# Order of the token tiles in layer 0's attention: context tiles between latent tiles

## The reference, cut to what matters

```python
for l in range(DEPTH):
    need_ctx = l < DEPTH - 1            # DEPTH = 2: layer 0 alone
    ...
    mix_x, mix_c = _token_mixers(px, pc, ...)
    h_x = _layer_norm(ALPHA * h_x + ga_x * (mix_x @ w_out[l]), ...)
...
# _token_mixers
o_a = _window_attn_latent(...)          # keys: 128 to either side, and the context, and a sink
o_b = _global_attn_latent(...)          # keys: all
o_d = _neigh_attn_latent(...)           # keys: all, with bias and mask
mix_c = concatenate([_dense_attn(a...), _dense_attn(b...), oc_ctx, _dense_attn(d...)])
```

## Time and profile before

| | |
|---|---|
| median of three runs | 2217.05 us |
| the profiled execution | 2221.32 us, its span 2219.5 us |
| busy share of the span | PE 92%, DVE 60%, ACT 33%, POOL 37% |
| attention of layer 0 | 453.1 us to 594.9 us |
| mean granted TensorE clock | 0.95 of full speed |

### The profile page before, as it was taken

One profiled execution on the slowest core, in us unless ns is written; L12 is line 12 of the kernel. 1 busy time (PEld: TensorE's weight loads), 2 busy tenths in 40 slices (PEclk: granted clock), 3 DMA queues, 4 the chain that ended last, 5 costly groups with the idle time before them and its releaser, 6 DMA issues.

```text
span 2219.5 us, 30665 instructions
## 1 busy us (share of the span) xinstructions
PE 2039.5 (92%) x11900; PEld 1641.9 (74%) x11900; DVE 1332.1 (60%) x2690; ACT 742.3 (33%) x1412; POOL 813.7 (37%) x620
## 2 busy tenths in 40 slices
PE   6998999989894999999989989999899969999897
PEld 3665877867682888888878867676777748888786
DVE  1028868676568799999843261875866762222445
ACT  2113343256611222222243311332336523333442
POOL 0005455220144243333353331444420354555553
PEclk9999998999996999999999999999799979999898
DMA  7541010110010333333321111111010102222321
GB/s 294 188 172 39 20 39 20 39 53 2 25 53 19 133 114 124 124 114 114 133 76 67 48 57 57 39 39 39 20 72 1 52 26 95 95 95 95 113 86 67
DMA packets 24128, 169.80 MB, mean 77 GB/s; under 512 B 2608, under 2 KB 2608, under 8 KB 4784
## 3 DMA queue, kind: packets, MB, share of 16 engines
q1 hardware_dynamic: 22544, 157.87, 19.7%
q10 hardware_dynamic: 1440, 9.96, 1.1%
HBM read 165.72 MB, written 2.10 MB: 76 GB/s over the span
## 4 chain that ended last, share of the span: by engine, by line
PE 76%; DVE 12%; issue 5%; POOL 4%; ACT 2%; DMA 1%; SPq 0%; POOLq 0%; DVEq 0%; ACTq 0%
PE PS L954 27%; PE PS L912 17%; PE PS L728 10%; PE PS L722 6%; PE PS L849 3%; PE PS L874 3%; PE PS L833 2%; PE PS L764 2%; DMA WR<-in_weights 1%; PE PS L839 1%; PE PS L649 1%; POOL W L1747 1%; DVE H L1611 1%; DVE H L1609 1%; PE PS L861 1%
## 5 line engine op out<-in xcount | busy, mean ns | idle before, releaser
L954 PE MATMUL PS<-XH,WS 128*128 128x512 f32 (+1 forms) x2112 | 571.4, 357 | 10.0 <-POOL WS L1785 6.9
L954 PEld LDWEIGHTS PS<-XH,WS 128*128 128x128 f32 x2112 | 378.5, 190 | 68.1 <-issue 9.7
L954 PE MATMUL PS<-XL,WS 128*128 128x512 f32 (+1 forms) x1056 | 376.1, 356 | 0.0
L1785 POOL TENSOR_TENSOR WS<-WR,WS 128x1024 fp32r<-128x1024 f32 x88 | 212.3, 2413 | 361.9 <-ACT WS L1163 361.9
L728 PE MATMUL PS<-WR,X 128*128 128x256 f32 x1248 | 290.5, 394 | 5.2 <-DMA WR<-in_weights 5.2
L728 PEld LDWEIGHTS PS<-WR,X 128*128 128x128 f32 x1248 | 245.4, 199 | 43.0 <-DMA WR<-in_weights 6.2
L1174 ACT ACTIVATE W<-PS,PR 128x768 f32<-128x768 f32 (+1 forms) x88 | 78.0, 886 | 464.5 <-PE PS L954 400.0
L954 PEld LDWEIGHTS PS<-XL,WS 128*128 128x128 f32 x1056 | 201.3, 191 | 28.2
L722 PE MATMUL PS<-X,WR 128*128 128x512 f32 (+1 forms) x576 | 209.1, 520 | 10.3 <-ACT U L1026 6.8
L1668 DVE SCALAR_TENSOR_TENSOR W<-PS,PR,W 128x511 f32<-128x511 f32 (+1 forms) x132 | 83.0, 656 | 217.1 <-ACT W L1174 217.1
L1250 DVE SCALAR_TENSOR_TENSOR W<-WR,SC,W 128x256 f32<-128x256 f32 x336 | 191.2, 610 | 6.0
(11 more groups left out here) (180 smaller groups left out, 3458.7 us busy)
## 6 DMA issues: line engine op xcount, KB each, us to landing
WR<-in_weights SPq DMA_DIRECT2D x144, 1024.0 KB, 4.8
W<-in_ln_rows ACTq DMA_DIRECT2D x4, 1024.0 KB, 4.6
U<-in_bias ACTq DMA_DIRECT2D x2, 1792.0 KB, 9.6
H<-in_x SPq DMA_DIRECT2D x1, 2048.0 KB, 10.4
WR<-in_weights SPq DMA_DIRECT2D x4, 512.0 KB, 3.5
out_h<-H ACTq DMA_DIRECT2D x4, 512.0 KB, 2.6
H<-in_ctx SPq DMA_DIRECT2D x1, 1024.0 KB, 12.5
PR<-in_params SPq DMA_DIRECT2D x1, 624.0 KB, 3.5
```

Source lines behind the costliest of these rows:

```text
L954: mm = pe.matmul(PS[u.pos][:, lo:hi], w[:, part, k, :], src[:, k, lo:hi], start=(k == 0 and src is xh3 and part == 0), stop=(k == KT - 1 a ...
L1785: pool.tensor_tensor(ws5[:, u.c % 2, 1], half_slot(u), ws5[:, u.c % 2, 0], ALU.subtract).then_inc(w_low, 1)
```

## The change

In layer 0 the tiles of each group are taken in the order 0, 4, 1, 5, 2, 3 instead of 0, 1, 2, 3, 4, 5. Layer 1 keeps its order.

```diff
         for l in range(DEPTH):
             for g in "ABD":
-                for t in range(tiles(l)):
+                for t in (0, 4, 1, 5, 2, 3) if has_ctx(l) else range(NLT):
                     for p in range(2):
```

## The result

The new order is slower: 2229.61 us, the median of six runs (2225.08 to 2231.45), against 2217.43 us (2216.51 to 2220.53, six runs). The ratio is 1.0050, with a 95% interval of 1.0038 to 1.0063, which is 11 us more, between 8.4 and 14; the medians themselves lie 12.2 us apart. I had forecast +3.2 us, at most 2223.5. The direction holds, the size doesn't, and what I called "can't be told from no change" can be told well.

The account below looks back on a forecast made before the run. TensorE, 92% busy, was taken to bound the kernel, with one large hole ended by GpSimd's L1758. 5.2 - 1.5 + 1.1 - 0.5 - 1.1 = +3.2 us gave 2220.3 us, range 2216.0 to 2223.5.

Parts of the forecast that it names:

- The wall: Layer 0, group A: VectorE's L1531, with two SBUF inputs, gets through only when GpSimd's L1758 lets go.
- the release: Group A: the moment GpSimd's L1758 lets VectorE's L1531 through, 8.29 us after L1515, ahead of the roots of job 5.
- T: End of the second L1508 in group A, 469.55 before, forecast 468.1; roots of job 5 start at T + 14.18.
- Work moved behind the release: Group A: scores, transposes and values of TensorE that ran ahead of the release now run behind it, +5.2 us.
- the release earlier: Group A: two context jobs instead of latent ones on VectorE bring T forward, -1.5 us, between 0 and 2.1 earlier.
- Seams, +1.1: Passages from a context tile to a latent one, groups A, B, D: 2.0 us new less 0.9 old.
- twice that: Upper bound set on the cost of seams from context to latent tiles, forecast between 0 and twice +1.1 us.
- Seams that go and the drain: Context pairs behind tile 4 no longer wait for maxima, -0.5 us; attention ends on latent tiles with less idleness, -1.1.
- The clock: The slow spell behind the release stays at about 1.4 us in both orders: 0, up to +1.5 us.
- slower by the clock: Rival, group A: clock falls to 1.2 GHz ahead of T, sum +4.7 to +6.9 us, from 2221.8; 13%.
- Everything behind attention is shifted and nothing else: Work after layer 0's attention only moves in time; layer 1 must look the same.
- slower by over 0.2%: Whole kernel: a time from 2221.5 us on, made of clock, L1515 late, part of the seams and the forecast's upper edge; 30%.

Follow-up runs that it names:

- Group A alone: The new order only in group A of layer 0, against the kernel before: ratio 1.0036 (1.0023 to 1.0049), attention 146.15 us, +4.3.
- late scaling: GpSimd's scaling of the bias table waits until group A's last sums are formed: 2210.24 us with the old order, 2215.10 us with the new.
- short exponentials: New order, late scaling, layer 0 group B exponentials over 64 columns without the maximum: 2215.15 us against 2215.10 with full ones; attention 140.26 against 141.57.
- run 20: Not a label of a run: part of "could run 20 us later", a verb and a time, said of an instruction on GpSimd.

## Why the prediction was wrong, step by step

- *The wall* (the release hangs on the second L1508 alone): right. 14.18 us from T to the roots in both orders, and without GpSimd's scaling beside it L1531 takes 0.16 us.
- *Work moved behind the release, +5.2; the release earlier, -1.5*: right. Group A alone cost +4.3 where the two, its seams and the clock sum to 4.1. From the roots of job 5 to L900 the new order takes 120.42 us against 111.19, 9.2 more; the moved work, the clock, the seams as measured below and the two gains at the end sum to 9.05.
- *Seams, +1.1*: the failed step. By distances in TensorE's rows the seams behind the release cost 0.6 in A, 3.2 in B and 1.9 in D, 5.7, where I had 2.0. Less the 0.9 of the old order's seams this is +4.8 and not +1.1. Two errors: I priced only the entry to a latent tile and nothing for the exit of a lone one, and in B's entry I let the waiting head take half of a pair's time, when alone it takes nearly all of it. My upper bound, "twice that", had the same blind spot: both rows it came from are seams with a second latent tile behind them, where the exit is covered. I also read D's row too low: not only the 0.29 of idleness counts but the 0.92 from 548.56 to 549.48 where four of twelve transposes take 0.49, so that such a seam costs 0.5 and not 0.37. That the exit hangs on the exponentials is shown by experiment; that the entry hangs on the maxima is read from rows. The two kernels with late scaling differ by 6.1 us of attention without a clock effect in either, 3.4 of it behind the roots of job 5, and short exponentials remove the exits in B, 1.3 us, the part that I had not priced.
- *Seams that go and the drain, -0.5 and -1.1*: right: the places where scores wait for maxima sum to 0.5 in the old order, and the drain equals layer 1's to a hundredth of a microsecond.
- *The clock, 0 to +1.5*: 0.65 inside attention, within bounds, but that is luck: one and the same hole was followed by 6.85 to 8.41 us for the same work. The bound covered only the place where the hole is. The rival "slower by the clock" put its price ahead of T, and there nothing was slow.
- *Everything behind attention is shifted and nothing else*: true of the instructions, wrong of the time. The profiled execution loses 2.95 us in the first projections of layer 1, and a bare delay of 7.8 us in the old order went with a rise of 10.6; why the clock is slow there in some kernels and not in others stays open.

In sum, attention: 3.2 forecast, 3.7 more by seams, 0.65 by the clock, 7.6 of 7.8 measured; the remaining 2.3 of the profiled execution are slow clock in identical work behind it, less the 0.85 won back. That the rest of the 11 us in the medians is the same thing is likely but not shown, as one execution was profiled. The chances were off as well: I gave 30% to "slower by over 0.2%", from 2221.5 on, while a doubled seam (+4.3) with a clock loss of 0.65 is already 2222.0.

## What to carry to other kernels

When light and heavy jobs share a software pipeline, look at each job with both neighbours: a heavy job is covered on entry by the job ahead of it and on exit by the one after it, and a row that shows one seam prices only that kind. Before reordering a pipeline around a long hole, find what ends the hole; here one instruction on GpSimd that could run 20 us later cost more than any order of the tiles that was tried won. And where the clock falls and rises again, allow for it before reading differences of some 3 us: here identical work took 2 to 3 us more in some kernels than in others, and no delay and no starting moment sorted them.

## What the runs showed of the hardware

- TensorE's products over half of the rows run beside each other when both halves come together: four passes of 512 columns take 0.96 us together (517.02 to 517.98), while one pass alone takes 0.43 (521.17 to 521.60).
- The same hole of 4.77 us was followed by a stretch at 1.2 GHz in eight kernels with the same instructions there; the work behind it took 7.17 us in one, 6.85 to 7.15 in three and 8.11 to 8.41 in four.
- GpSimd's `tensor_scalar` over 3584 columns takes 9.28 us beside group B and 10.05 when it starts 0.06 behind L1515. VectorE's 128x4 `tensor_tensor` with both inputs in SBUF, issued while it runs, takes 5.63 to 6.89 us instead of 0.16 and ends 8.28 or 8.29 behind L1515's end; reductions of VectorE that read PSUM and one tensor of SBUF run at their usual 0.48 us beside it.
